# Single-tile first norm, smaller constants ahead of the first weights, and the router's products amid the conditioning's: a two-block kernel on one core

## The reference

```
h    = rms_norm(x, norm1_g);  proj = h @ w_in            # first norm, first projection
...    attention, LRU and convolution branches, w_out, residual
h2   = rms_norm(x, norm2_g)
logits_c = h2 @ w_coarse;  logits_f = h2 @ w_fine          # router: a group of 4, then 2 of its 8 experts
order = argsort(expert of each assignment)                 # tokens gathered by expert
y[t] += gate * ((silu(xe @ w_gate[e]) * (xe @ w_up[e])) @ w_down[e])
...
m = silu(cond) @ ada_w + ada_b                             # conditioning of the second block, two layers, two conditions
```

## Time and profile before

| | |
|---|---|
| median of 3 runs | 2342.57 us (2339.99 to 2343.46) |
| the profiled execution | 2337.69 us |
| its span in the profile | 2335.9 us |
| TensorE busy | 2166.2 us, 93% of the span |
| VectorE, ScalarE, GpSimd busy | 58%, 44%, 16% |
| mean granted TensorE clock | 0.975 of full |
| DMA | 348.76 MB, mean 149 GB/s |
| chain that ended last | TensorE 76%, VectorE 10%, DMA 7%, ScalarE 5% |

### The profile page before, as it was taken

The page is one execution under the profiler, slowest core; times in us unless marked ns, Lnnn a source line. Parts: engine busy times, 40 slices in busy tenths (PEclk is TensorE's granted clock), DMA queues, the critical chain, the costliest instruction groups (busy, mean ns, idle before and its releaser), DMA issues.

```text
span 2335.9 us, 26485 instructions
## 1 busy us (share of the span) xinstructions
PE 2166.2 (93%) x10595; PEld 1547.6 (66%) x10595; DVE 1352.4 (58%) x1727; ACT 1027.7 (44%) x1509; POOL 365.1 (16%) x263
## 2 busy tenths in 40 slices
PE   6999999898699998998879999988999999899998
PEld 5877755574585665665568777744555567788886
DVE  5687277453875475474473255566555556543385
ACT  3265366511575465464453234345444523412231
POOL 2000012000210110110100000012555633000014
PEclk9999999998899999999989999999999999999999
DMA  4111030117899999999763011130000031211041
GB/s 128 55 51 40 28 127 28 72 67 300 316 389 412 410 396 394 401 390 406 303 224 84 19 40 29 45 115 1 1 37 1 19 135 73 84 37 54 20 180 64
DMA packets 105743, 348.76 MB, mean 149 GB/s; under 512 B 21944, under 2 KB 54593, under 8 KB 79632
## 3 DMA queue, kind: packets, MB, share of 16 engines
q1 hardware_dynamic: 94896, 321.70, 36.2%
q0 software_dynamic: 9504, 21.08, 2.4%
q10 hardware_dynamic: 1216, 4.24, 0.5%
HBM read 323.21 MB, written 34.26 MB: 153 GB/s over the span
## 4 chain that ended last, share of the span: by engine, by line
PE 76%; DVE 10%; DMA 7%; ACT 5%; issue 2%; SPq 0%; POOL 0%; DVEq 0%; ACTq 0%; POOLq 0%
PE psm L236 72%; DMA mem<-in_exp_w_gate_dram 2%; DVE small L3455 2%; DMA mem<-in_exp_w_up_dram 2%; DVE r L350 1%; PE psm L1109 1%; PE psm L1973 1%; ACT mem L1191 1%; ACT r L341 1%; DMA mem<-in_ada_w_dram 1%; PE psm L483 1%; DMA mem<-in_w_in_dram 1%; PE psm L2019 1%; DMA mem<-in_odd_w_out_dram 1%; DVE mem L3160 0%
## 5 line engine op out<-in xcount | busy, mean ns | idle before, releaser
L236 PE MATMUL psm<-r,r 128*128 128x512 f32 (+3 forms) x6449 | 1545.6, 396 | 76.0 <-DVE r L2140 15.1
L236 PEld LDWEIGHTS psm<-r,r 128*128 128x128 f32 (+2 forms) x6449 | 1191.4, 190 | 414.1 <-issue 92.5
L350 DVE TENSOR_TENSOR r<-mem,r 128x1024 fp32r<-128x1024 f32 (+1 forms) x312 | 360.0, 1198 | 248.5 <-ACT r L341 245.3
L236 PE MATMUL psm<-mem 128*64 128x512 f32 (+11 forms) x2870 | 465.2, 449 | 24.5 <-DMA mem<-in_ada_w_dram 13.5
L341 ACT ACTIVATE r<-mem 128x1024 fp32r<-128x1024 f32 (+1 forms) x312 | 301.5, 1025 | 136.7 <-DMA mem<-in_exp_w_gate_dram 50.8
L236 PEld LDWEIGHTS psm<-mem 128*64 128x64 f32 (+5 forms) x2870 | 205.5, 152 | 222.4 <-issue 162.4
L3669 POOL TENSOR_TENSOR mem<-mem 128x1024 f32<-128x1024 f32 x63 | 152.6, 2421 | 161.8 <-ACT mem L3621 107.1
L3621 ACT ACTIVATE mem<-psm 128x512 f32<-128x512 f32 x160 | 94.4, 595 | 142.1 <-PE psm L236 135.5
L3455 DVE TENSOR_REDUCE small<-psm 128x1 f32<-128x1280 f32 x64 | 95.3, 1488 | 86.5 <-PE psm L236 86.5
L1239 DVE TENSOR_TENSOR_SCAN mem<-mem,small 128x128 f32<-128x128 f32 (+7 forms) x64 | 83.7, 1356 | 24.3 <-POOL mem L1255 20.1
L271 ACT ACTIVATE small<-small 128x1 f32<-128x1 f32 (+2 forms) x31 | 9.1, 294 | 200.6 <-DVE small L387 123.6
(11 more groups left out here) (370 smaller groups left out, 1673.2 us busy)
## 6 DMA issues: line engine op xcount, KB each, us to landing
mem<-in_exp_w_gate_dram SPq DMA_DIRECT2D x64, 1024.0 KB, 8.3
mem<-in_exp_w_up_dram SPq DMA_DIRECT2D x64, 1024.0 KB, 8.7
mem<-in_exp_w_down_dram SPq DMA_DIRECT2D x64, 1024.0 KB, 9.9
mem<-in_ada_w_dram SPq DMA_DIRECT2D x32, 768.0 KB, 13.5
mem<-in_odd_w_in_dram SPq DMA_DIRECT2D x10, 1024.0 KB, 5.6
mem<-in_x_dram SPq DMA_DIRECT2D x16, 512.0 KB, 6.2
mem<-in_w_in_dram SPq DMA_DIRECT2D x8, 1024.0 KB, 5.3
mem<-y2d SPq DMA_DIRECT2D x8, 1024.0 KB, 7.2
```

The costliest lines, as they stand in the source:

```text
L236: return p.e.matmul(o, l, r, start=start, stop=stop, skip_group_check=True)
L350: p.e.tensor_tensor(l, mem(self.raw(i), [R * n])[:, w * q:w * q + w], h.bitcast(F32), SUB).then_inc(*self.lo_done.up(i, q))
```

## The change

SP sends the identity (128 columns, 64 KB) alone after x tile 0, and the rest of the constants after x tile 7. GpSimd sends `g1` at once and its other small transfers after x tile 3 has landed. The first half of the first norm goes tile by tile: statistics, root and scaling of one tile before the next, and a new `turn_rows_tensor` turns tile by tile into eight banks of PSUM. TensorE waits for the identity at its start, and for the rest of the constants before it turns the columns.

In the router's stage conditioning blocks 5 to 8 move from ahead of the router's products to behind them, with block 9 between them and the table as before, and blocks 10 and 11 behind the table. On VectorE the lo split of the first expert piece moves behind the table, and `order_vector` from inside the expert stage to right behind the table, ahead of all splits.

```
+            def turn_rows_tensor(self, p, half, order=ALL):
+                blocks = self.blocks(half)
+                banks_ = [take(p, self.name, q, c, order=order) for q, c, _ in blocks]
+                for i in self.part(half):
+                    p.wait_ge(*(self.dve if i % 2 else self.act).at("norm", i))
+                    for (q, c, _), ps in zip(blocks, banks_):
+                        j = i - self.g * q
+                        last = p.e.transpose(ps[:, 128 * j:128 * j + 128], self.tmp[i][:, c::8], cst("ident"))
+                        if i == self.part(half)[-1]:
+                            last.then_inc(*self.pe.up(q, c))
...
         def prologue_sync(p):
             for i in range(NT):
                 p.e.dma_start(XIN[i], xs[:, i, :]).then_inc(*x_in[i].up("x"))
-                if i == 3:
-                    p.e.dma_start(CS[:, :], A["k_small"][:, 0:NC - 256]).then_inc(*consts_in.up())
+                if i == 0:
+                    p.e.dma_start(CS[:, 0:128], A["k_small"][:, 0:128]).then_inc(*ident_in.up())
+                elif i == 3:
                     WI.fetch(p, 0)
+            p.e.dma_start(CS[:, 128:NC - 256], A["k_small"][:, 128:NC - 256]).then_inc(*consts_in.up())
         def prologue_pool(p):
             p.e.dma_start(g1, ...).then_inc(*g1_in.up())
+            p.wait_ge(*x_in[3].at("x"))
...
         def norm1_scalar(p):
-            n1.stats_scalar(p, 0)
-            n1.norm_scalar(p, 0)
+            for i in range(4):
+                n1.stats_scalar(p, (i,))
+                n1.norm_scalar(p, (i,))
...
         def norm1_vector(p):
-            n1.stats_vector(p, lambda i: [x_in[i].at("x")], 0)
-            n1.norm_vector(p, 0)
+            for i in range(4):
+                n1.stats_vector(p, lambda i: [x_in[i].at("x")], (i,))
+                if i >= 2:
+                    n1.norm_vector(p, (2 * i - 3,))
...
         def project_tensor(p, lru, conf):
-            n1.turn_tensor(p, 0)
+            n1.turn_rows_tensor(p, 0)
...
                     n1.turn_tensor(p, 1)
+                    p.wait_ge(*consts_in.at())
                     rows_tensor(p)
...
         def norm2_tensor(p):
-            ada_tensor(p, 0, 9)
+            ada_tensor(p, 0, 5)
...
         def table_vector(p):
-            WE.split_vector(p, 0)
             p.wait_ge(*rt_pe.at("tab"))
...
-            for i in range(1, 3):
+            order_vector(p)
+            for i in range(3):
                 WE.split_vector(p, i)
...
         def experts_vector(p):
             turn_vector(p, 0)
-            order_vector(p)
...
         def tensor(e):
-            p.wait_ge(*consts_in.at())
+            p.wait_ge(*ident_in.at())
...
             router_tensor(p)
-            ada_tensor(p, 9, 12)
+            ada_tensor(p, 5, 10)
             table_tensor(p)
+            ada_tensor(p, 10, 12)
             experts_tensor(p)
```

More of the change, by code:

```diff
@@ L524, in build @@
         consts_in, columns_in, gates_in, g1_in = load("consts_in"), load("columns_in"), load("gates_in"), load("g1_in")
+        ident_in = load("ident_in")
         x_in = [load(f"x{i}_in") for i in range(NT)]
```

## The result

The changed kernel takes 2323.23 us, the median of 4 runs (2321.99 to 2325.65), against 2341.28 (2336.46 to 2343.46) for the kernel before. The medians differ by 18.05 us or 0.77%; the ratio taken over all runs is 0.9928 with a 95% interval of 0.9914 to 0.9942, that is 16.9 us (13.6 to 20.1). I had said 2332.0, with a range of 2327 to 2338. One execution of the kernel before, beside the first experiments, took 5230.16 us and counts in no ratio. The two profiled executions differ by 14.1 us (spans 2335.9 and 2321.8; 2337.69 and 2323.56 us with what lies around).

A forecast was written before the change was run, and what follows sets the result against it. TensorE, busy for 93% of the span, was taken to bound the kernel, with time won only at its waits: start 2.9 plus router 7.7 gives 10.6 us, so 2332.0 against a median of 2342.57; range 2327 to 2338.

The forecast's parts named there:

- three signs of being wrong: First weights landing past 17 us, TensorE waiting for VectorE's operands at the table, first gather taking over 12 us.
- the gather's contention: Router: first gather and perhaps half the second go ahead of the third expert piece, 1.4 and 0.7 us.
- The start, 2.9 us: Start: first weights no longer queue behind 600 KB of constants and land at 15.1 us, 2.9 us earlier.
- Rival (a): Start gives nothing because the small loads now slow the first weights; 2334.9 us, chance 0.15.
- Does anything else come late?: Start, behind the weights' landing: turned chunks needed at 17.1 us, there by 17.5 at most; at worst 0.4 us.
- TensorE's warmth: Start: turns in short pieces may leave the first products at the lower clock, 2.5 us lost but hidden by VectorE.
- The router's products, 15.4 us earlier for VectorE: Router: products behind block 4 let VectorE go on at 569.0 instead of 584.4 us, 15.4 us earlier.
- The table's 3.57 us: Router: the table takes 3.57 us behind block 9 and ends at 589.4 instead of 602.3 us.
- rival (b): Router: first gather stands behind all queued weights, so the router gives only 0.9 us; 2338.8 us, chance 0.10.
- (c): Start and router: weights land at 14.1 us and no contention, gain 13.7 us; 2328.9 us, chance 0.13.
- (d): From 40.24 us on: short turns leave TensorE cold far beyond the first products, slower; 2349.0 us, chance 0.03.
- (e): Downstream: the gain is absorbed at a wait for DMA; 2341 us, chance 0.05.

The follow-up runs named there:

- identity second: Changed kernel with the identity's transfer behind x tile 1 instead of behind tile 0; ratio to the kernel before 0.9948 (0.9928 to 0.9968).
- small loads free: Changed kernel without GpSimd's wait for x tile 3, its small loads again beside x tiles 0 to 3; ratio to the kernel before 0.994.
- whole gathers: Changed kernel with empty slots of a block gathering row 1023, so each gather moves 128 rows; one run, 2335.20 us.

## Why the prediction was wrong

It named the right places and the right direction, and none of its three signs of being wrong came. What failed is one term of the sum, the gather's contention, sized at 2.1 us where the trace has 0.16, and the 2 us that it gave to the spread of runs. Its 10.6 us became 14.4 in the traces: 0.4 more at the start, 2.0 more in the router, of which 1.9 are that contention, and 1.4 between them that no part of the change made. The rest of the way to 18 us is in no place of the traces and most likely spread of the runs. By its own steps:

- *The start, 2.9 us.* Measured 3.28 us in the first two traces, 2.75 between the means of the three profiles with the old start and the six with the new one (35.90 and 33.14), and 3.8 in the timed runs of that part alone. The size was right and the cause mostly not, so that it came out was luck. I gave the 2.9 us to the 600 KB and let the small loads count for nothing. The runs show the reverse: with the 600 KB put back the split is at 15.13, with the small loads put back at 16.88, in the changed kernel at 14.6 to 14.8. Rival (a), which rested on the small loads slowing the first weights, did not happen: GpSimd issued them from 10.74 on, when the weights' transfers were well on their way, and the weights were in before ScalarE was free at 14.75. Put back to the start, they do slow them. The trace has 24 small loads, 15 of columns and 8 of gate weights behind the gain, where I had counted 22.
- *"Does anything else come late?"* Yes, and I had it as level at worst. VectorE's chain from tile 1 is the bound now. With the identity's transfer ahead of it that tile is taken up at 6.85 to 8.30 in six profiles instead of 5.9 to 6.1, and with the identity second at 6.21 and 6.35. I had looked only for the turned chunks, and not for the roots of tile 3 that stand ahead of the weight split in ScalarE's queue. It is inside what the forecast allowed.
- *TensorE's warmth.* As forecast, though smaller: the products took 12.80 us instead of 11.17, 1.6 us more where I had priced 2.5, at a clock of 0.50 from 20 to 22 us, and VectorE's chain hid it (turns behind them at 33.23, waiting for VectorE).
- *From 40 us to the router: moved along.* Nearly. The lead is 3.13 us up to 416 us and 4.72 at the logits (554.23 to 549.51). The 1.6 us come from one short stretch at the lower clock that the profile of the kernel before has and that of the changed kernel has not (columns of rows 3, first before, then after):

```profile
416.00:422.00 6.00, 5.71 (x36) 3.62 (x37) 1.39 (x2) 2.87 (x5) 0.00 (x0) 0.72 0.00 0
```

```profile
412.90:418.90 6.00, 5.75 (x40) 3.57 (x41) 1.36 (x2) 2.85 (x5) 0.00 (x0) 1.00 0.00 0
```

- *The router's products, 15.4 us earlier for VectorE.* VectorE took them up 30.17 us behind the logits' turn before (584.40 less 554.23) and 14.49 after (564.00 less 549.51), 15.7 us earlier. Right.
- *The table's 3.57 us.* Mis-sized. It ran at the upper clock and took 1.96 us, ending at 583.2. With the gather off the path this is worth nothing through the gather, whose rows were turned 2.3 us ahead of the third piece's landing. But a table that ran 3.60 us, with blocks 10 and 11 slower behind it, held back the fetches of the expert pieces and gave a distance of 52.0 (small loads free).
- *The gather's contention, 2.1 us.* This is the step of the router that failed. I priced each gather at 128 rows, 0.52 MB, and it moves at most 0.16, because empty slots fetch nothing. The third piece landed 45.26 us behind the logits, where it did before (599.33 less 554.23, 45.10): 0.16 us of contention. That is the whole of 9.7 - 7.7. The experiment with whole gathers gives 1.4 us back, so it was the bytes that I had wrong more than their price. That a gather goes between the weights and not behind them was right: it landed 7.1 us after its issue at 585.38, so rival (b) is out.
- *Rivals.* (c), 13.7 us, was nearest for the traces: no contention, but by 0.5 us less at the start. (d) and (e) did not happen: the 14.40 us at the first product were 14.1 at the end.
- *The range.* The sum of the two steps in the traces is 13.0 us (3.3 + 9.7), with the missing stretch 14.1 to 14.4; 2342.57 less that is 2328.3, inside the range. The other 5 us to 2323.23 are in no place of the traces. They are most likely spread of the runs: the profiled execution of the kernel before, 2337.69, was 3.6 us faster than the median of its series (2341.28), that of the changed kernel 0.3 slower than its own, which turns 14.1 into 18. The base of 2342.57 was itself 1 to 2 us above the later medians, and the changed kernel's own medians are 4.4 us apart. No experiment separates that from a gain that the two traces miss. I had given 2 us for the spread of runs where a median of four needs some 4. What decides which short stretches an execution has stays open, and the stretch near 417 us, missing from the changed kernel's first profile, is luck and not part of the change.

## What to carry to other kernels

When two engines' queues move past each other, ask which transfer is next behind the one removed and how many bytes it really moves: here a gather with a bound on its rows moved 0.16 MB and not 0.52. A chain that waits behind an in-order queue is worth what lies between it and the next thing that lands, here 9.7 of 15.7 us, since the third weight piece set the rest; shortening it further gave an earlier first product and no shorter stage. And where a change moves a fraction of a per cent, price the spread of medians too, by a second series, and read the gain from points in the traces.

## What was not expected of the hardware

Fifteen small loads of columns from GpSimd's queue, 48 KB in all, went with 16 DMA engines that were busy for only 0.51 to 0.73 from 6 to 10 us, in all four profiles that have them there, while SP's queue had megabytes waiting. In the nine profiles without them the same 4 us were at 0.95 to 1.11. Small loads free against changed shows that they are the cause; how they do it stays open.

TensorE's granted clock falls to its lower level for short stretches in places that differ from one execution of a kernel to the next: the 29 turns took 3.48 us in one execution and 5.11 in the other. Such a stretch on TensorE's path cost 1.6 us there. That their number is what makes single executions of one kernel differ by several us (the part behind the expert stage took 1161.9 and 1165.1 us in the two profiles of the kernel before, 1161.9 and 1165.4 in those of the changed kernel) is likely and not shown.
